# Three more input projections by seven products instead of eight, in a one-core hybrid decoder layer

## The reference

```python
mod = jax.nn.silu(c) @ ada_w + ada_b
sh1, sc1, g1, sh2, sc2, g2 = jnp.split(mod[:, None, :], 6, axis=-1)
h = _rms(x, norm1_g) * (1.0 + sc1) + sh1
z = h @ w_in                      # 16 groups of 512 columns and some gates
y_m = mlstm_mixer(m_q, m_k, m_v, m_o, ...)
y_b = moba_mixer(b_q, b_k, b_v, ...)      # q and k are RMS-normed per head
y_r = retention_mixer(r_q, r_k, r_v, r_g, ...)
y_n = nsa_mixer(n_q, n_kc, n_vc, n_ks, n_vs, n_kw, n_vw, ...)
x = x + g1 * (concatenate([y_m, y_b, y_r, y_n]) @ w_out)
h2 = _rms(x, norm2_g) * (1.0 + sc2) + sh2
return x + g2 * hier_moe(h2, ...)         # 32 experts, top 1 group, top 2 inside it
```

## Time and profile before

| | us |
|---|---|
| time, median of 3 runs | 1665.14 (1665.05 to 1674.46) |
| the profiled execution | 1668.25, of which the span of the trace is 1666.1 |
| busy in the span: TensorE | 1393.0 (84%) |
| busy: VectorE / ScalarE / GpSimd | 595.8 / 187.7 / 31.4 |
| stage 1, 2, 3, 4 begin at about | 0, 134, 617, 747 |
| DMA over the span | 611.90 MB, mean 367 GB/s |

### The profile page before, as it was taken

The page is one execution under the profiler, slowest core; times in us unless marked ns, Lnnn a source line. Parts: engine busy times, 40 slices in busy tenths (PEclk is TensorE's granted clock), DMA queues, the critical chain, the costliest instruction groups (busy, mean ns, idle before and its releaser), DMA issues.

```text
span 1666.1 us, 17839 instructions
## 1 busy us (share of the span) xinstructions
PE 1393.0 (84%) x7389; PEld 760.7 (46%) x7389; DVE 595.8 (36%) x927; ACT 187.7 (11%) x459; POOL 31.4 (2%) x35
## 2 busy tenths in 40 slices
PE   5998999979999999998876776777677667767767
PEld 4666888758556854473422322223223223223223
DVE  4556684676445457422211221121120121122113
ACT  2001221102012100121100100100100101001001
POOL 0000000000000000010000000000000000000000
PEclk9999999989999999999988887787788788787788
DMA  9996686667758677869999999999999999999997
GB/s 397 427 426 259 251 342 272 257 246 280 268 220 328 234 291 299 361 253 421 424 429 428 428 429 428 429 429 428 428 428 428 428 429 428 428 429 429 428 429 293
DMA packets 44536, 611.90 MB, mean 367 GB/s; under 512 B 4896, under 2 KB 5168, under 8 KB 6736
## 3 DMA queue, kind: packets, MB, share of 16 engines
q1 hardware_dynamic: 42848, 604.00, 87.5%
q0 software_dynamic: 1072, 6.44, 0.9%
q10 hardware_dynamic: 576, 0.89, 0.1%
HBM read 609.21 MB, written 2.10 MB: 367 GB/s over the span
## 4 chain that ended last, share of the span: by engine, by line
PE 49%; DMA 45%; DVE 5%; issue 1%; ACT 0%; SPq 0%; POOL 0%; DVEq 0%
DMA ring<-in_exp_w 31%; DMA Zpad<-in_exp_w 10%; PE W L671 8%; PE W L658 7%; PE W L650 7%; PE M L1092 5%; PE W L1000 5%; DMA ring<-in_stream 3%; PE W L624 2%; PE A L1110 2%; PE W L1044 2%; DVE tail L1441 2%; PE W L976 2%; PE M L634 2%; PE W L1057 2%; PE M L1064 1%
## 5 line engine op out<-in xcount | busy, mean ns | idle before, releaser
L1441 DVE SCALAR_TENSOR_TENSOR tail<-ring,small,tail 128x512 f32<-128x512 f32 x300 | 225.6, 752 | 10.5
L1092 PE MATMUL M<-ring,g1b 128*32 128x512 f32 x1024 | 148.3, 711 | 62.9 <-DMA ring<-in_exp_w 62.9
L1374 DVE TENSOR_TENSOR consts<-A,tail 32x512 f32<-32x512 f32 x128 | 87.9, 686 | 162.5 <-PE A L1110 159.5
L658 PE MATMUL W<-ring,buf_h 128*128 128x512 f32 x320 | 140.7, 598 | 0.0
L1952 DVE SCALAR_TENSOR_TENSOR tail<-tail,M 128x128 f32<-128x128 f32 x32 | 9.2, 288 | 295.6 <-ACT tail L1351 295.6
L1110 PE MATMUL A<-Zpad,tail 128*32 128x512 f32 x512 | 84.5, 793 | 36.3 <-DMA Zpad<-in_exp_w 31.9
L650 PE MATMUL W<-buf_h,ring 128*128 128x256 f32 x512 | 112.0, 379 | 0.2 <-DMA ring<-in_stream 0.2
L1064 PEld LDWEIGHTS M<-consts,tail 128*128 128x128 f32 x512 | 68.4, 208 | 92.1 <-ACT tail L1353 60.0
L650 PEld LDWEIGHTS W<-buf_h,ring 128*128 128x128 f32 x512 | 96.7, 190 | 13.3 <-issue 0.4
L1092 PEld LDWEIGHTS M<-ring,g1b 128*32 128x32 f32 x1024 | 30.8, 119 | 146.5 <-DMA ring<-in_exp_w 90.4
L1092 PE MATMUL M<-Zpad,g1b 128*32 128x512 f32 x512 | 74.9, 713 | 27.0 <-DMA Zpad<-in_exp_w 27.0
(11 more groups left out here) (311 smaller groups left out, 1301.0 us busy)
## 6 DMA issues: line engine op xcount, KB each, us to landing
ring<-in_stream SPq DMA_DIRECT2D x88, 2048.0 KB, 10.3
ring<-in_exp_w SPq DMA_DIRECT2D x88, 2048.0 KB, 38.3
Zpad<-in_exp_w SPq DMA_DIRECT2D x64, 2048.0 KB, 32.1
PPY<-in_exp_w SPq DMA_DIRECT2D x24, 2048.0 KB, 30.8
tail<-in_exp_w SPq DMA_DIRECT2D x16, 2048.0 KB, 45.2
Zpad<-in_early SPq DMA_DIRECT2D x8, 1536.0 KB, 10.6
buf_x<-in_x SPq DMA_DIRECT2D x2, 1024.0 KB, 7.0
buf_h<-in_x POOLq DMA_DIRECT2D x1, 2048.0 KB, 12.3
```

The lines of the kernel that those rows point to most:

```text
L658: ins = pe.matmul(dst[:, tt * 512:tt * 512 + 512], hT[:, kk, tt * P:tt * P + P], w[:, 512 * k:512 * k + 512], start=(kk == 0), stop=(kk == ...
L1092: ins = pe.matmul(M[32 * j:32 * j + 32, 512 * w13:512 * w13 + 512], XT[:, kk, 32 * q:32 * q + 32], w[:, 512 * k:512 * k + 512], start=(kk ...
L1374: return dve.tensor_tensor(o, x, y, op)
L1441: ins = dve.scalar_tensor_tensor(acc, w, cs[:, kk:kk + 1], acc, ALU.mult, ALU.add)
```

## The change

- `SEVEN` gets `r_v`, `b_q` and `b_k`: they take seven products; their weights are stored by column halves as for the others.
- Buffers: `sum_3` is `g1b` for the `n_` chunks and the free convolution buffer `pad` for the others, so GpSimd's load of the gate bias into `g1b` moves from after `b_v`'s product 4 to after `n_vw`'s. The mixers' output takes `buf_x` columns 1024 to 2047 before the last chunks are done; the token sum that lies there is now `S4`, and ScalarE moves it to a free slot (`slot_5`, one 128x1024 copy) in `m_decay`; products 5 of the three new chunks read it there.
- `ORDER`: sums and corners for the three chunks; `pv slc` in front of `sums_31 m_o`; `m_decay` behind `ada 15` and `sums_31 r_v`; `ada` blocks earlier; the mLSTM step `m_pv` is split, and its VectorE part, `m_out`, stands behind `sums_24 b_k`.
- `place_sums`: the finishing steps are held back behind the `ada` and `sums_31` that follow a chunk.
- `EARLY_CORNERS`: `n_ks` makes copies 0, 1 and 2 in `sums_24`, ahead of ScalarE's `gates` work. `early b_k`: copies 1 and 2 of `b_k` ahead of `turn b_q`. `FIRST_PRODUCTS`: four of `b_k`'s products in the first half.

```diff
+EARLY_CORNERS = {'n_ks': 3, 'm_o': 2}
+FIRST_PRODUCTS = {'b_k': 4}
+SEVEN = ('n_ks', 'n_vs', 'n_kw', 'n_vw', 'm_o', 'b_v', 'r_v', 'b_q', 'b_k')
...
+         ('chunk', 'm_v'), ('ada', 13), ('pv', 'slc'), ('sums_31', 'm_o'), ('sums_24', 'm_o'), ('scores', 'win'),
...
     for step, arg in order:
+        if step not in ('ada', 'sums_31'):
+            placed += due
+            due = []
         placed.append((step, arg))
...
         elif step == 'chunk':
-            placed += waiting
+            due = waiting
             waiting = [('ada_turn', b) for s, b in waiting if s == 'ada_rows']
...
-        S1, S2, S3, S4 = (h_sums[:, i] for i in range(4))
+        S1, S4, S2, S3 = (h_sums[:, i] for i in range(4))
+        S4_later = slot_5.rearrange("p (k t) -> p k t", k=8)
...
+                    elif i == 5:
+                        if name == 'r_v':
+                            pe.wait_ge(sem["sums_moved"], 1)
+                        pe.wait_ge(sem["corner_copied"], 5 * s + 3)
+                        product(r2, S4_later if name in ('r_v', 'b_q', 'b_k') else S4, w22, False).then_inc(
+                            sem["products_done"], 1)
...
                     copy_corner(arg, 0)
-                    if arg == 'm_o':
-                        copy_corner(arg, 1)
+                    for i in range(1, EARLY_CORNERS.get(arg, 1)):
+                        copy_corner(arg, i)
...
+                elif step == 'early':
+                    copy_corner(arg, 1)
+                    copy_corner(arg, 2)
...
                     act.activation(PA, PA, ACT.Exp).then_inc(sem["m_decay_ready"], 1)
+                    act.activation(slot_5, h_sums[:, 1].rearrange("p k t -> p (k t)"), ACT.Copy).then_inc(
+                        sem["sums_moved"], 1)
```

More of the change, by code:

```diff
@@ L79 @@
          ('chunk', 'm_k'), ('turn', 'n_kw'), ('ada', 12), ('turn_p', 'slc'), ('conv', 'm_k'),
-         ('chunk', 'm_v'), ('ada', 13), ('sums_31', 'm_o'), ('pv', 'slc'), ('sums_24', 'm_o'), ('scores', 'win'),
+         ('chunk', 'm_v'), ('ada', 13), ('pv', 'slc'), ('sums_31', 'm_o'), ('sums_24', 'm_o'), ('scores', 'win'),
          ('chunk', 'm_o'), ('ada', 14), ('sums_31', 'b_v'), ('turn_p', 'win'), ('sums_24', 'b_v'), ('pv', 'win'),
[L82 to L85, removed]
+         ('chunk', 'b_v'), ('ada', 15), ('sums_31', 'r_v'), ('m_decay', 0), ('sums_24', 'r_v'), ('turn_y', 'n'),
+         ('chunk', 'r_v'), ('ada', 16), ('sums_31', 'b_q'), ('m_scores', 0), ('sums_24', 'b_q'),
+         ('chunk', 'b_q'), ('ada', 17), ('sums_31', 'b_k'), ('m_pv', 0), ('sums_24', 'b_k'), ('norm', 'b_q'),
+         ('m_out', 0), ('early', 'b_k'), ('turn', 'b_q'),
+         ('chunk', 'b_k'), ('ada', 18), ('corners', 'b_k'), ('turn_y', 'm'), ('norm', 'b_k'), ('turn', 'b_k'),
          ('chunk', 'r_q'), ('scores', 'moba'), ('ada', 19), ('turn_p', 'moba'),
@@ L105, in place_sums @@
         elif step == 'chunk':
-            placed += waiting
+            due = waiting
             waiting = [('ada_turn', b) for s, b in waiting if s == 'ada_rows']
-    assert not waiting
+    assert not waiting and not due
     return placed
@@ L124, in order_of_pe @@
             waiting = []
-        elif step not in ('sums_31', 'sums_24', 'corners'):
+        elif step not in ('sums_31', 'sums_24', 'corners', 'early', 'm_out', 'norm'):
             assert not waiting or step == 'conv'
@@ L525, in _ @@
                     rsqrt(rst).then_inc(sem["norm_rstd"], 1)
-                elif (step, arg) == ('corners', 'b_v'):
-                    pool.wait_ge(sem["products_done"], products_before('b_v') + 4)
+                elif (step, arg) == ('corners', 'n_vw'):
+                    pool.wait_ge(sem["products_done"], products_before('n_vw') + 4)
                     pool.wait_ge(sem["late_loaded"], 16)
@@ L530, in _ @@
                         sem["late_loaded"], 16)
-                elif step in ('m_pv', 'r_pv'):
+                elif step in ('m_out', 'r_pv'):
                     pool.wait_ge(sem[f"y_{step[0]}_ms"], 1)
@@ L685, in seven_products @@
[L685 to L692, removed]
@@ L1182, in _ @@
                         act.wait_ge(sem["o_done"], 1)
+                    elif arg == 'r_v':
+                        act.wait_ge(sem["o_done"], 2)
+                    elif arg in ('b_q', 'b_k'):
+                        act.wait_ge(sem["m_scores_done"], 1)
                     copy_corner(arg, 0)
[L1184 to L1186 removed]
+                    for i in range(1, EARLY_CORNERS.get(arg, 1)):
+                        copy_corner(arg, i)
+                    if arg == 'b_v':
                         act.wait_ge(sem["chunk_copied"], chunk_no('m_o'))
                         act.activation(zslot['m_o'], zslot['m_o'], ACT.Tanh, scale=0.5).then_inc(sem["gate_tanh_m"], 1)
+                elif step == 'early':
+                    copy_corner(arg, 1)
+                    copy_corner(arg, 2)
                 elif step == 'chunk' and arg in SEVEN:
[L1190 removed]
+                    for i in range(3 if ('early', arg) in ORDER else EARLY_CORNERS.get(arg, 1), 5):
                         copy_corner(arg, i)
@@ L1193, in _ @@
                     z = zslot[arg]
-                    done = [n for n in SEVEN if ORDER.index(('sums_24', n)) < ORDER.index((step, arg))]
-                    act.wait_ge(sem["chunk_copied"], chunk_no(arg))
-                    if arg in EARLY or done[-1] in ('n_vw', 'b_v'):
-                        act.wait_ge(sem["chunk_copied"], chunk_no(done[-1] if done[-1] in ('n_vw', 'b_v') else done[-2]))
-                    else:
-                        act.wait_ge(sem["chunk_copied"], chunk_no(done[-2]))
+                    done = [n for n in SEVEN if corners_step(n) < ORDER.index((step, arg))]
+                    act.wait_ge(sem["chunk_copied"], max(chunk_no(arg), chunk_no(done[-1])))
                     for i in range(8):
@@ L1747, in _ @@
                     tt_op(PB, M[:], PA, ALU.mult).then_inc(sem["m_p_ready"], 1)
-                elif step == 'm_pv':
+                elif step == 'm_out':
                     dve.wait_ge(sem["enm_ready"], 1)
```

65 lines of the change are left out of this document (39 added, 26 removed).

## The result

| | before | changed |
|---|---|---|
| median of 4 runs each, us | 1669.49 (1665.05 to 1674.46) | 1641.86 (1640.05 to 1652.74) |
| profiled execution / span of its trace | 1668.25 / 1666.1 | 1640.05 / 1638.3 |
| TensorE enters `w_out` | 617.40 | 591.34 |
| first expert matmul | 752.61 | 726.84 |

The ratio is 0.9848, with a 95% interval of 0.9805 to 0.9891. In the two traces TensorE is 26.1 us ahead at `w_out` and 25.8 at the first expert. What follows was 2.0 us shorter, which the change didn't touch.

The account below looks back on a forecast made before the run. TensorE was taken to bound the kernel up to the expert stream, DMA in stage 4. 7.9 + 9.8 + 3 x 3.3 - 1.6 - 1.9 = 24.1 us less than 1665.1 gave 1641.0 us, range 1634 to 1651.

Parts of the forecast that it names:

- The bound: TensorE's time up to the expert stream moves the end one for one; stage 4 is DMA's, of fixed length.
- n_ks: Stage 2, before product 4: the 5.15 us hole and the slow work behind it go; 7.9 us saved.
- m_o: Stage 2: the 9.62 us hole before scores win goes, product 2 then needs the third weight sum; 9.8 us saved.
- The new chunks: r_v, b_q and b_k: seven products each save 3.3 us per chunk.
- The covers: New work stays hidden: by 1.7 us at r_v, 1.2 at b_q, 3 for norm b_q, 0.9 for norm b_k.
- ada_sum 16: Ahead of m_pv and b_k: TensorE waits 2.2 us for VectorE's turn where it waited 0.62; -1.6 us.
- I leave this in: First half of r_v, right behind m_decay: its slow piece of 1.8 us stays.
- The clock at the new waits: Slow work behind two new waits of some 2 us, at m_o and ada_sum 16; bounds 0 and 3.7, -1.9 taken.
- No slow clock: Rival: no slow work at the new waits; 1639.1 us, or 1637 with a smaller ada_sum wait; chance 0.13.
- VectorE as the bound: Rival: VectorE bounds the last three chunks; 1650.9 us if it takes each 3.3, 1644 if a third; chance 0.18.
- no gain: Rival: the expert stream is bound by something that starts on its own; 1665 us; chance 0.05.
- slower: Rival: TensorE waits whole rounds of 25 us at ada_sum 16, 17 and 18; 1689 us; chance 0.04.

Follow-up runs that it names:

- the corners: Kernel before with one edit: ScalarE makes copies 0, 1 and 2 of n_ks ahead of its gates work; 1666.61 us.
- the swap alone: Kernel before with one edit: pv slc stands in front of sums_31 m_o; 1669.35 us.
- the turn put first: Changed kernel with ada_turn 1 and ada_sum 16 on VectorE again in front of sums_31 b_k; 1640.79 us, 0.9841 of before.
- with the copies: Changed kernel with the moved token sum copied four times instead of once by ScalarE in m_decay; 1642.44 us.
- two products: Changed kernel with only two of b_k's products in the first half, ahead of turn b_q, instead of four; 1652.97 us.
- more sums: Changed kernel with one more 128x2048 pass on VectorE in sums_31 of r_v and of b_q; 1652.54 us.
- changed, again: Changed kernel without an edit, run once more on another chip; 1648.56 us, 0.9877 of before.

## Why the prediction was right, and where it wasn't

**The bound.** Right. Every microsecond of the mark arrived at the first expert matmul (26.06 and 25.77), and what follows kept its length to 2.0 us. But stage 4 isn't the block of fixed length that the prediction took it for, nor is it all DMA's: its first 65 us run at TensorE's pace, and up to 6.6 us of the spread arise up to there. The 8 us of spread behind the mark are as much as the corners brought. That the predicted median (1641.0) and the measured one (1641.86) agree to 0.9 us is therefore partly luck. The same kernel gave 1648.56 elsewhere. The ratios, 0.9848 and 0.9877, are the result; 0.9855 was forecast.

**`n_ks`.** Right, 7.96 and 8.10 for 7.9, clock included.

**`m_o`.** Right in size (9.88 for 9.8) and in what comes next: product 2 waits for the third sum. Wrong in where TensorE stands: its scores ran at full speed and left a wait of 2.31 us. The two possibilities were in the text and give the same start. The prediction didn't say which edit does it. It is `place_sums`; the swap alone moves the wait from the scores to product 2, and beside `place_sums` all that it gains is the slow piece of `r_v` (606.06 for 607.91).

**The new chunks.** Right: 3.30 and 3.29 us at `b_q` and `b_k`, and `r_v` 3.3 beside the slow piece. With the turn put first, they bring 29.24 - 19.38 = 9.9 us, all of 3 x 3.3. The covers held: 1.7 us computed on ScalarE and 1.7 measured. Ahead of `turn b_q` the norm's cover was right (2.9 for 3), but VectorE's read of `M`, with 2.4, was nearer. At `b_q`, 1.2 was computed on VectorE, and 2.3 more work made no wait at its product 2: VectorE stood idle before that for DMA and TensorE, and the added work went into those gaps. A cover that is worked out from an engine's end, without its waits, is a lower bound.

**`ada_sum 16`.** Right in mechanism; the term was too small, 2.69 us for 2.2. VectorE's path was landing, two sums, turn, as written; the landing is what varies (8.8 to 9.6 us over five traces, 8.3 forecast). It could have been avoided by one condition, and the working shows it: the turn takes 0.6 us and needs nothing that the sums make.

**`m_decay`.** Wrong. "I leave this in" took the slow piece for a property of `m_decay`'s four-row matmuls. It wasn't: the same matmuls had full speed behind them in every kernel with the swap, and 1.7 us came as an unforeseen gain. Nearly all of the 2.0 us by which the sum was short (24.1 for 26.06) is this.

**The clock at the new waits.** The size chosen, 1.9, was near to what the first trace shows (1.6), and as a term it failed. "The bounds are 0 and 3.7" were taken from one slow piece each; in the five traces that have both waits the runs show 1.6 to 8.3 for the two together. That the choice came near is luck:

| wait on TensorE | slow work behind it, us |
|---|---|
| 2.3, `m_o`, five traces | 0 |
| 2.3, `m_o`, three traces | 1.7 each |
| 2.69, `ada_sum 16`, with the copies | 0 |
| 2.69, `ada_sum 16`, changed kernel | 1.6 |
| 2.97, `ada_sum 16`, two products | 1.7 |
| 3.37, `ada_sum 16`, more sums | 6.6 |
| 3.48, `ada_sum 16`, changed, again | 7.6 |
| 3.86, product 2 of `m_o`, swap alone | 2.5 |
| 4.46, before `turn b_q`, two products | 2.4 |
| 0.62, `ada_sum 16`, nine traces | 0 |
| 1.4 and then 0.3, before the first expert, nine traces | 0 |
| the same, five traces | 1.5 to 1.6 each |

(Slow work is TensorE's time for a piece less that of the same piece at granted clock 1.00, 6.35 us for `ada_sum 16` with `m_pv` and 13.92 for the four products behind.) The Trainium skill ("TensorE: Matmul & The Clock Gate", HAM oscillation) lays the slow clock to idle gaps. For `ada_sum 16` the runs agree: a gap of 0.62 us, no slow work, and bringing the gap down to that was worth 10.3 us against one execution and 3.2 against another. It is not the whole rule: the same gap was followed by none or by 1.7 us, and `r_v`'s slow half had no gap ahead of it.

**The rivals.** "No slow clock" came true at `m_o`, and in the copies' kernel at `ada_sum 16`. VectorE as the bound, no gain, and slower: none of them is seen in any trace of the changed kernel. No wait at `ada_sum 17` or `18` appeared.

## What to carry to other kernels

A wait of 2 to 3.5 us on TensorE can be dearer than it looks, and by an amount that differs from run to run: behind it stood between none and 7.6 us of slow work here. Find what stands ahead of the small result that ends it, and move that result first. When an edit swaps the order of two steps on a late engine, ask for both consumers: the swap moved a wait here, and only more work done in the engine's idle time removed it. Judge edits of a few microseconds piece by piece in the trace: the whole time of one kernel moved by 6 us between two traces, and the start of a later stage by 7, with no edit at all. And before a mean rate is called the stream's speed, cut the window smaller and ask whose pace the chain follows there.

## What the hardware showed

- The same instructions behind the same wait of 2.69 us ran at a granted clock of 1.00 in one trace and 0.92 in another; behind waits of 3.37 and 3.48 us at 0.69 and 0.63. 1.00 is the 2.4 GHz level. One of `m_pv`'s matmuls came every 0.22 us there and every 0.43 in the slow stretch, which is the 1.2 GHz level.
- A slow piece of 1.7 us without a gap ahead of it came in every trace with one order of VectorE's steps and in none with the other, 50 us later than the swapped steps. What links them isn't known.
- The full expert stream ran at 428 to 429 GB/s from 1100 to 1460 us in all fourteen traces. Where the mean fell to 421 in an earlier stretch, it was one slice of 20 us at 333, while the chain was on TensorE and that at a granted clock of 0.91.
